# Differential attention: combining the two probability maps in two parts, each with its own signal

## What is computed

```
s = einsum('bhcqd,bhckd->bhcqk', qb, k) * scale        # c = 0, 1: two maps
p = softmax(where(mask, s, -inf), axis=-1)
a = p[:, :, 0] - lam_val * p[:, :, 1]
o = einsum('bhqk,bhkv->bhqv', a, v)                    # then rmsnorm(o) * (1 - lam_init)
```

## Time and profile before

| | |
|---|---|
| median of three runs | 2237.4 us (2237.3 to 2239.85) |
| the profiled execution's own time | 2239.56 us |
| its span in the trace | 2237.8 us |
| mean granted TensorE clock, share of full speed | 0.998 |
| PE busy | 2208.1 us, 99% of the span |
| PEld busy | 1836.4 us, 82% |
| DVE busy | 1638.5 us, 73% |
| ACT busy | 973.3 us, 43% |
| POOL busy | 874.3 us, 39% |
| the DMA queue's share of 16 engines | 40.9% |

### The profile page before, as it was taken

The page is one execution under the profiler, slowest core; times in us unless marked ns, Lnnn a source line. Parts: engine busy times, 40 slices in busy tenths (PEclk is TensorE's granted clock), DMA queues, the critical chain, the costliest instruction groups (busy, mean ns, idle before and its releaser), DMA issues.

```text
span 2237.8 us, 28701 instructions
## 1 busy us (share of the span) xinstructions
PE 2208.1 (99%) x10501; PEld 1836.4 (82%) x10501; DVE 1638.5 (73%) x2141; ACT 973.3 (43%) x1613; POOL 874.3 (39%) x805
## 2 busy tenths in 40 slices
PE   8999999999999999999999999999999999999998
PEld 6888888888888888888888888877888888888887
DVE  6877776599669478399577777786599569388397
ACT  6354454354244243345254445564354243343346
POOL 4945546200234233230866666675201234232320
PEclk9999999999999999999999999999999999999999
DMA  8677743463551632701522222222463542633601
GB/s 256 217 269 259 244 155 99 139 246 113 188 188 43 254 128 103 269 13 38 160 67 66 66 66 66 66 76 76 160 230 109 200 176 75 245 113 123 234 0 76
DMA packets 139844, 317.37 MB, mean 142 GB/s; under 512 B 8609, under 2 KB 82514, under 8 KB 126546
## 3 DMA queue, kind: packets, MB, share of 16 engines
q1 hardware_dynamic: 137552, 315.78, 40.9%
q10 hardware_dynamic: 2178, 0.06, 0.1%
HBM read 242.41 MB, written 56.62 MB: 134 GB/s over the span
## 4 chain that ended last, share of the span: by engine, by line
PE 95%; DVE 3%; ACT 1%; issue 1%; DMA 0%; ACTq 0%; DVEq 0%
PE aps L1317 10%; PE aps L1321 10%; PE aps L1319 10%; PE mps L1317 4%; PE dps L1317 4%; PE mps L1321 4%; PE dps L1321 4%; PE mps L1319 4%; PE dps L1319 4%; PE dps L1183 4%; PE dps L1185 4%; PE dps L1184 4%; PE dps L1201 3%; PE dps L1203 3%; PE dps L1202 3%; PE mps L1676 2%
## 5 line engine op out<-in xcount | busy, mean ns | idle before, releaser
L1317 PE MATMUL aps<-b_ring,w_hi 128*128 128x512 f32 x640 | 249.3, 390 | 0.0
L1321 PE MATMUL aps<-b_ring,w_hi 128*128 128x512 f32 x640 | 249.0, 389 | 0.0
L1319 PE MATMUL aps<-b_ring,w_lo 128*128 128x512 f32 x640 | 249.0, 389 | 0.0
L1031 POOL TENSOR_TENSOR s_blk<-s_blk,a 128x1024 f32<-128x1024 f32 x24 | 68.6, 2860 | 380.1 <-DVE w_lo L2520 253.8
L2538 DVE TENSOR_TENSOR b_ring<-h,b_ring 128x1024 fp32r<-128x1024 f32 x120 | 206.5, 1728 | 5.6 <-ACT b_ring L1914 5.6
L909 POOL TENSOR_TENSOR w_hi<-w_raw,ones 128x256 fp32r<-128x256 f32 (+1 forms) x133 | 122.7, 952 | 201.1 <-PE dps L1203 103.9
L1023 POOL TENSOR_TENSOR s_blk<-a,a22u 128x1024 f32<-128x1024 f32 x12 | 35.5, 2960 | 325.6 <-DMA a<-in_w_up 318.6
L1317 PE MATMUL aps<-b_ring,a_hi 128*128 128x512 f32 x384 | 149.8, 390 | 0.0
L1319 PE MATMUL aps<-b_ring,a_lo 128*128 128x512 f32 x384 | 149.4, 389 | 0.0
L1321 PE MATMUL aps<-b_ring,a_hi 128*128 128x512 f32 x384 | 149.4, 389 | 0.0
L1317 PEld LDWEIGHTS aps<-b_ring,w_hi 128*128 128x128 f32 x640 | 120.1, 188 | 25.4 <-issue 0.7
(11 more groups left out here) (514 smaller groups left out, 6362.5 us busy)
## 6 DMA issues: line engine op xcount, KB each, us to landing
b_ring<-xs SPq DMA_DIRECT2D x42, 2048.0 KB, 7.9
xs<-b_ring SPq DMA_DIRECT2D x14, 2048.0 KB, 7.9
one_hi<-xm SPq DMA_DIRECT2D x19, 1024.0 KB, 5.0
one_lo<-xm SPq DMA_DIRECT2D x19, 1024.0 KB, 7.3
a<-in_w_up SPq DMA_DIRECT2D x16, 1024.0 KB, 5.3
a<-in_w_down SPq DMA_DIRECT2D x16, 1024.0 KB, 7.9
w_raw<-in_diff_w_in SPq DMA_DIRECT2D x24, 512.0 KB, 4.0
mix_a<-in_mlstm_w_in SPq DMA_DIRECT2D x36, 256.0 KB, 7.8
```

Of the source, the lines that this page charges most:

```text
L1317: nc.tensor.matmul(to[:, n], wh, ring[:, 0, k], start=new and k == 0, stop=False, skip_group_check=not new)
L1319: nc.tensor.matmul(to[:, n], wl, ring[:, 0, k], start=False, stop=False, skip_group_check=not new)
L1321: last = nc.tensor.matmul(to[:, n], wh, ring[:, 1, k], start=False, stop=(k == 3), skip_group_check=not new)
```

## The change

`combine` now waits for map 0's exponentials alone, takes the reciprocal of the first sum and the product lam * r0, and only then waits for map 1's. What is left behind the second wait is one reciprocal, one product of two columns, and the pass. For rows of four or more tiles (m >= 3) the pass is cut in two: the first three tiles, and the rest. Each part ends with its own signal on `comb_ready`, so that semaphore counts 13 in a head rather than 8 (`COMBINED`), and PE waits for the second part before the second batch of transposes. The chain on DVE has one link more in each row.

```
+COMBINED = 2 * NB - 3
...
+    def combined(hd, m, part):
+        return COMBINED * hd + m + max(m - 3, 0) + part + 1
...
             def values(hd, m, feed, between, early=lambda: None):
-                pe.wait_ge(comb_ready, n + 1)
+                pe.wait_ge(comb_ready, combined(hd, m, 0))
...
+                    if t == 1:
+                        pe.wait_ge(comb_ready, combined(hd, m, 1))
                     if u >= 2:
                         pe.wait_ge(t_out, BATCH * hd + u - 1)
...
             def combine(hd, m):
                 n, w = 8 * hd + m, P * (m + 1)
+                dve.wait_ge(exp_done, 2 * n + 1)
+                nc.vector.reciprocal(small[:, 11, m:m + 1], small[:, 9, m:m + 1])
+                ch.link(nc.vector.tensor_scalar(small[:, 1, m:m + 1], small[:, 9, m:m + 1], lamc[:, 0:1], None, ALU.mult))
                 dve.wait_ge(exp_done, 2 * n + 2)
-                nc.vector.reciprocal(small[:, 11, m:m + 1], small[:, 9, m:m + 1])
                 ch.link(nc.vector.reciprocal(small[:, 0, m:m + 1], small[:, 10, m:m + 1]))
-                ch.link(nc.vector.tensor_scalar(small[:, 1, m:m + 1], small[:, 0, m:m + 1],
-                                                small[:, 9, m:m + 1], lamc[:, 0:1], ALU.mult, ALU.mult))
-                nc.vector.scalar_tensor_tensor(ee[:, 0, 0:w], ee[:, 1, 0:w], small[:, 1, m:m + 1],
-                                               ee[:, 0, 0:w], ALU.mult, ALU.add).then_inc(comb_ready, 1)
+                ch.link(nc.vector.tensor_tensor(small[:, 1, m:m + 1], small[:, 1, m:m + 1], small[:, 0, m:m + 1], ALU.mult))
+                for cut in [slice(0, min(w, 3 * P)), slice(3 * P, w)][:1 if m < 3 else 2]:
+                    nc.vector.scalar_tensor_tensor(ee[:, 0, cut], ee[:, 1, cut], small[:, 1, m:m + 1],
+                                                   ee[:, 0, cut], ALU.mult, ALU.add).then_inc(comb_ready, 1)
...
-            PER_HEAD = 2 + 4 * NB + RSQRT_LINKS
+            PER_HEAD = 2 + 5 * NB + RSQRT_LINKS
```

## The result

| | before | after |
|---|---|---|
| median of 17 runs each, same chip | 2238.08 us (2237.15 to 2242.66) | 2242.16 us (2240.02 to 2245.29) |
| ratio, 95% interval | | 1.0016 (1.001 to 1.0023) |
| the profiled execution, its span | 2239.56, 2237.8 | 2244.0, 2242.0 |
| granted TensorE clock | 0.998 | 0.996 |
| DVE busy | 1638.5 | 1675.2 |

What follows compares the result with a forecast made beforehand. PE, busy nearly the whole span, bounds the kernel; the edit can aim only at its 6.9 us of waits for DVE's combining pass. -0.1 - 0.24 + 0 = -0.35 us takes the median 2237.4 to 2237.0, range 2234.3 to 2239.9.

Steps and rivals of the forecast that it cites:

- the sum for heads 6 and 7: DVE and ACT loop: each combine from row 3 on saves 0.06 us, -0.24 in head 6; head 7 taken as 0.
- The third rival: Second pass delays `q_lo`: +2.5 us, 2239.9, chance 12%, of which 3% with POOL's 0.5 us slowdown in every head, over 2242.
- the -0.1 us for heads 0 to 5: Six regular heads: about 0.02 us kept in each, -0.1 us in all, with 0 and -0.4 as ends.
- the chain: DVE, regular head, last exponentials to pass: 0.38 us instead of 0.57, saving 0.19.
- both passes in row 7: DVE, regular head: 384 and 640 columns take 1.33 us together, 0.13 more than the one pass.
- PE's gain at the transposes: Row 7 of regular heads: PE's fourth transpose starts 0.4 us earlier, lost again at `q_lo`.
- The handover: Next head's first scores wait for the last `q_lo` transfer, already at its limit; DVE's `split_q` sets its issue.
- a kept 0.02 a head: Regular heads: gain kept through an earlier `q_lo` landing, 0.06 us if it follows the issue, 0 if transfers collide.
- The named waits of 0.2 to 0.4 us for `q_lo`: Sign expected in the new trace: PE's first scores of heads 1 to 6 show a named wait of 0.2 to 0.4 us.
- 0.06 earlier: Regular heads: `split_q` starts 0.06 us earlier after the last exponential, 0.19 saved less 0.13 for the second pass.
- prediction's own signs of being wrong: Forecast counts as wrong if heads get shorter by 0.2 us or more, or if `split_q` starts later.
- Head 7: Rows 0 and 2 lose 0.19 us net each, row 1 and rows 3 to 7 give back: -0.1 to +0.2, taken as 0.

Runs made afterwards that it cites:

- e6: Changed kernel with POOL's work from head 6 on cut to 8 of 256 columns and its next-stage input split put off: 2239.13 us, ratio 1.0 to before.
- e5: Kernel before with POOL's work from head 6 on cut to 8 of 256 columns and its next-stage input split put off: 2236.64 us, ratio 0.9989.
- e7: Kernel before with three chained one-column reciprocals between row 7's pass and `split_q` in heads 0 to 5: 2240.19 us, ratio 1.0002.
- e9: Changed kernel with the `w_raw` loads in heads 1, 3 and 5 waiting until `q_lo` has landed: 2242.31 us, ratio 1.0012 to before.
- e13: Kernel before with only PE's second wait in rows 3 to 7 added, on a value reached long before: 2238.73 us, ratio 1.0.
- e2: Changed kernel with the new chain of small operations but no cut of the pass: ratio 1.0001 to before.
- e3: Changed kernel without cuts, the product of two columns made a tensor_scalar with one tensor input: ratio 1.0005 to before.
- e14: Kernel before with the pass cut in two in rows 3 to 7 of head 7 alone, old chain, POOL as before: 2238.33 us, ratio 1.0.
- e1: Changed kernel with the cuts kept and the old chain of small operations restored: ratio 1.0014 to before.
- e8: Kernel before, old chain, with the pass cut in two in heads 6 and 7: 2241.54 us, ratio 1.0009.
- e10: Kernel before with POOL's split of the next stage's first weight panel waiting for the last `split_q`: 2244.16 us, ratio 1.002.

## Why the prediction was wrong, step by step

**The step that failed** is the sum for heads 6 and 7: "Each combine of a row from 3 on shortens the loop by 0.06." It priced a second pass at 0.13 us by the earlier trace rows, passes that were not held. In rows 5 to 7 of head 6 POOL hardly rests and DVE is on the path. There a second pass costs its own hold, 0.46 to 0.47 us in each of the three rows, and so does the new product (0.16 became 0.35, 0.66 and 0.39). The two passes took 0.5 to 0.8 us more than the one. Forecast -0.24 for head 6, measured +2.29; e6 against e5 gives what is left without POOL, +0.46. The row that said so stood in the prediction, 1.79 against 1.28 us in the earlier trace rows, and I used to say that it "isn't met" at row 7 of head 0, which is true there, and then carried the undisturbed price into the head where a hold is paid for. The third rival named that slowdown, with 3%, but as 0.5 us for every head: in the regular heads the holds fall into rows 0 to 6, where DVE mostly has room, and head 6 pays for several. That its price, over 2242, lies beside the 2242.16 measured is luck.

The other term that failed is the -0.1 us for heads 0 to 5: they took 1.15 us more, 0.77 of it in head 0 and 0.38 at the handovers of heads 1 to 5. Head 6 makes 2.3 of the 3.5 us.

**Right:** the chain (0.39 for 0.38), both passes in row 7 (1.34 for 1.33), PE's gain at the transposes (0.25 to 0.35 us for 0.4) and that it would not be kept: in heads 1 to 5 the time from row 7's transposes to the next first scores rose from 7.53 to 7.74 and more.

**The handover** was read too simply. I took `split_q` as what moves the landing, with the landing at the limit. e7 shows that in heads 2 and 4 a `split_q` 0.7 us later moves nothing: the copies behind each other land at the same time, and PE's own stream ends then too. I had read the 0.14 and 0.19 us between the first two score matmuls as a held load; the rows before them (feed matmuls 0.23 apart up to the first scores) would have shown that PE came without any pause. The forecast of a kept 0.02 a head, 0.06 at most, was too small for heads 2 and 4 (-0.11 and -0.15) and wrong in sign for the odd ones (+0.33, +0.21 and +0.10), where `w_raw`'s loads take part (e9). The named waits of 0.2 to 0.4 us for `q_lo` at the first scores of heads 1 to 6 are there in part, and hardly in name: PE's pause is 0.2 to 0.4 us at heads 2, 4 and 6 and 0.01 to 0.03 at heads 3 and 5, from the distance of the starts, and only head 1's (0.77), head 7's and one other are named.

**`split_q`** starts 0.02 us later in head 0 and 0.02 to 0.14 later in heads 1 to 5, counted from the head's first scores, not 0.06 earlier; a later `split_q` was one of the prediction's own signs of being wrong. In head 0 the reciprocal that opens the chain starts at 43.84 instead of 43.76. The chain behind it is shorter as forecast.

**Missed altogether:** the wait for ACT's squares ahead of row 7's transposes, which takes over there; and the +0.77 us in head 0 that come with PE's longer code (e13); how that code costs them is open. The prediction priced PE's register instructions at nothing, which holds for their own time.

**Head 7:** 0 forecast, +0.09 measured. In parts: the chain costs 0.5 to 0.6 there (e2, e3; 0.38 forecast for rows 0 and 2), and the cut alone 0.33 (e14), so the two didn't add up, and the same cuts gave -0.4 to -0.6 behind a longer head 6 (e1, e8). Head 7's length depends on when it begins, which I didn't separate further.

## What to carry to other kernels

Before a DVE operation with two SBUF inputs is cut in two, look at what POOL is doing at each place where the new instruction will stand, and price it from a row of that place: a second pass that cost 0.13 us in row 7 of head 0 cost 0.5 to 0.8 in rows 5 to 7 of head 6. A wait of the busiest engine that lies ahead of a meeting point can be halved without a gain; look at the rows just before the meeting point, to see whether the engine arrives with or without a pause, and delay each candidate to see which one sets it. Compare a long kernel by stages: ahead of the attention the profiles scatter by 5 us, more than the whole effect.

## What the runs showed of the hardware that I had not expected

- A DVE operation of one column with two SBUF inputs takes 0.16 us beside an idle POOL and up to 0.77 beside a busy one; the same product with a scalar pointer in place of the second tensor isn't held (e3: 212 to 216 ns for all 64 of the kernel; the product's mean over head 6 is 342 in the changed kernel).
- A hold doesn't grow with the width of the pass: 0.44 us at 128 columns (0.79 against 0.35), 0.27 at 896 and 0.50 at 1024, and 0.62 at most in all profiles.
- Of four copies of 256 KB in a row, the last one issued 0.7 us later took 0.7 us less (4.45 to 3.75), with the DMA engines over 90% busy with these copies from 48.0 to 51.8 us into the head.
- With one wait more on PE in each of rows 3 to 7 (e13), a packet of 16 KB of instructions came at 51.3 instead of 55.1 us behind head 0's first scores, in among `q_lo`'s copies, and head 0 took 0.8 us more.
- A pause of PE of 4.8 us (e10) was followed by a granted clock of 0.50 for some 6 us.
